# Routing stage of an encoder block on one core: when GpSimd folds, where ScalarE's exponentials and TensorE's turned picks stand

## The reference, cut to what matters

```
h    = x + mixed @ W_out;  xb = rmsnorm(h)
q    = (xb @ w_q)                                   # 8 heads x 2 halves x 64
s    = q . sub_keys                                 # 16 rows of 128 scores a token
s_top, i_top = top_k(s, 16)                         # 16 best of each row
best, pos    = top_k(sums of the two halves, 16)    # 16 best pairs a head
expert = i_top[first half] * 128 + i_top[second half] at pos
gate   = softmax(best)
```

## Time and profile before

| | |
|---|---|
| device time, median of 3 runs | 5196.68 us (5194.86 to 5203.18) |
| the profiled execution: its own time, its span | 5196.66 us, 5195.0 us |
| VectorE's first sum of `route` to its last copy on ScalarE | 2156.0 to 2702.6 us of the span |
| first marks of block 0 and of block 9 (L1968) | 2248.1 and 2677.9 us |
| from the marks of block 0 to those of block 7, a block | 49.0 us |
| blocks 8 and 9, a block | 43.5 us |

### The profile page before, as it was taken

One profiled execution on the slowest core, in us unless ns is written; L12 is line 12 of the kernel. 1 busy time (PEld: TensorE's weight loads), 2 busy tenths in 40 slices (PEclk: granted clock), 3 DMA queues, 4 the chain that ended last, 5 costly groups with the idle time before them and its releaser, 6 DMA issues. The chain is left out here.

```text
span 5195.0 us, 68977 instructions
## 1 busy us (share of the span) xinstructions
PE 4512.5 (87%) x23172; PEld 3713.1 (71%) x23172; DVE 3660.1 (70%) x7429; ACT 1535.4 (30%) x2729; POOL 2239.4 (43%) x1840
## 2 busy tenths in 40 slices
PE   7999998455599979977619679999999999999999
PEld 6888887344244448655518578889899899888898
DVE  2000000778477822288989689999999999999999
ACT  3111100455367732111109622222222222222221
POOL 4222211345245501034357555555555555665554
PEclk9999999677799989988859889999999999999999
DMA  4222211110311143200006799999999899999998
GB/s 136 82 82 82 90 61 40 51 40 10 136 62 68 42 156 120 89 33 29 29 25 183 233 352 329 339 335 339 337 336 337 318 342 337 328 326 337 333 336 295
DMA packets 376378, 978.51 MB, mean 188 GB/s; under 512 B 31097, under 2 KB 155801, under 8 KB 375961
## 3 DMA queue, kind: packets, MB, share of 16 engines
q0 software_dynamic: 156416, 575.12, 30.3%
q1 hardware_dynamic: 218688, 397.83, 22.7%
q10 hardware_dynamic: 1152, 4.19, 0.2%
HBM read 858.96 MB, written 116.75 MB: 188 GB/s over the span
## 5 line engine op out<-in xcount | busy, mean ns | idle before, releaser
L2368 PE MATMUL e_ph<-e_x,e_u 128*128 128x384 f32 x6144 | 1202.0, 337 | 67.5 <-DVE e_x L2433 52.5
L2368 PEld LDWEIGHTS e_ph<-e_x,e_u 128*128 128x128 f32 x6144 | 1097.8, 189 | 140.2 <-POOL e_u L2341 41.9
L2390 PE MATMUL e_po<-e_v,e_w 128*128 128x512 f32 x3840 | 998.4, 396 | 19.9 <-DVE e_v L2466 12.9
L2348 POOL DMA_INDIRECT e_row<-in_v_exp,expert_tok x512 | 624.7, 1220 | 468.1 <-DVE e_tok L2493 412.9
L2390 PEld LDWEIGHTS e_po<-e_v,e_w 128*128 128x128 f32 x3840 | 712.0, 188 | 140.2 <-DVE e_v L2466 13.2
L2348 POOL DMA_INDIRECT e_row<-in_u_rows,expert_tok x512 | 594.4, 1161 | 475.3 <-DVE e_row L2482 428.3
L324 PE MATMUL proj_acc<-xn,w_tile 128*128 128x512 f32 (+1 forms) x3456 | 678.1, 358 | 5.3 <-POOL w_tile L354 5.3
L2493 DVE SCALAR_TENSOR_TENSOR e_tok<-e_row,e_slot,e_tok 128x1024 f32<-128x1024 f32 x512 | 648.3, 1271 | 12.7 <-DMA e_tok<-h_tok_dram 9.2
L324 PEld LDWEIGHTS proj_acc<-xn,w_tile 128*128 128x128 f32 x3456 | 575.4, 188 | 107.8 <-POOL w_tile L354 5.5
L2482 DVE SCALAR_TENSOR_TENSOR e_row<-e_row,e_tok 128x1024 f32<-128x1024 f32 x512 | 618.9, 1213 | 7.5 <-DMA e_row<-in_u_rows,expert_tok 7.3
L284 DVE COPY proj_out<-proj_acc 128x1280 f32<-128x1280 f32 x25 | 37.3, 1492 | 659.9 <-PE proj_acc L324 647.5
(11 more groups left out here) (314 smaller groups left out, 6827.7 us busy)
## 6 DMA issues: line engine op xcount, KB each, us to landing
e_u_raw<-in_u_exp SPq DMA_DIRECT2D x128, 512.0 KB, 6.6
e_v_raw<-in_v_exp SPq DMA_DIRECT2D x128, 512.0 KB
gates_dram<-g_out SPq DMA_DIRECT2D x6, 8192.0 KB, 30.3
e_g<-gates_dram SPq DMA_DIRECT2D x128, 384.0 KB, 6.5
feat_dram<-proj_out POOLq DMA_DIRECT2D x50, 640.0 KB, 5.8
w_raw<-in_w_feat SPq DMA_DIRECT2D x50, 512.0 KB, 4.9
raw<-feat_dram SPq DMA_DIRECT2D x22, 640.0 KB, 6.1
mx_gate<-feat_dram SPq DMA_DIRECT2D x16, 640.0 KB, 4.0
```

The costliest lines, as they stand in the source:

```text
L2348: pool.indirect_dma_start(out=row[r % RB][:], out_offset=None, in_=u_rows if r < TOK_ROWS else v_rows, in_offset=bass.IndirectOffsetOnAxis ...
L2368: ins = nc.tensor.matmul(ph[q % 2][:, 0:tn], u[b][j][:, kk, :], xs[m][:, kk, t0:t0 + tn], start=(i == 0), stop=(i == 3 * DC - 1))
L2390: ins = nc.tensor.matmul(out, w[b][j][:, blk * P:(blk + 1) * P], v[2 * odd + b][m][:, half * HALF:(half + 1) * HALF], start=(n == 0 and (f ...
```

## The change

Three edits, all in `route`. GpSimd waits for both sets of marks of block n before it folds the first. ScalarE takes the exponentials of block n behind `scale_features(n + 2)` in its round n, rather than those of block n-1 at the start of the round, and copies the turned picks behind both halves of the queries. TensorE does both halves of the queries before it turns the picks. No instruction is added or removed.

```diff
                 for n in range(TB):
+                    pool.wait_ge(marked[1], n + 1)
                     for j, rows in ((0, slice(0, 8)), (1, slice(8, 16))):
                         pool.wait_ge(marked[j], n + 1)
...
                 for n in range(TB):
-                    if n:
-                        gates_of(n - 1)
                     if n + 2 < TB:
                         root(n + 2)
                         scale_rows(n + 2)
                         scale_features(n + 2)
-                        keep_queries(n + 2, 0)
+                    gates_of(n)
+                    if n + 2 < TB:
+                        for half in range(2):
+                            keep_queries(n + 2, half)
                     if n:
                         keep_turned(n - 1)
-                    if n + 2 < TB:
-                        keep_queries(n + 2, 1)
-                gates_of(TB - 1)
                 keep_turned(TB - 1)
...
                     if n + 2 < TB:
                         turn_rows(n + 2, 1)
-                        queries(n + 2, 0)
+                        for half in range(2):
+                            queries(n + 2, half)
                     if n:
                         turn(n - 1)
-                    if n + 2 < TB:
-                        queries(n + 2, 1)
                 turn(TB - 1)
```

## The result

The changed kernel takes 5104.06 us (median of 4 runs, 5103.15 to 5109.79) where the kernel before, in the same comparison, took 5195.77: a ratio of 0.9825, with a 95% interval of 0.9808 to 0.9842. The profiled execution has 5103.16 us and a span of 5101.5 us.

What follows compares the result with a forecast made beforehand. A circle of waits through TensorE, ScalarE's exponentials and VectorE, 48.81 us, was taken to bound the kernel. First to last marks 94.8 us less, 1.6 lost at the end: 93.2 off 5196.66 gives 5103.5 us, range 5093 to 5120.

Steps and rivals of the forecast that it cites:

- the circle: Waits through TensorE, ScalarE's exponentials and VectorE, 48.81 us round, set the pace of seven blocks; VectorE's marks lie outside it.
- The marks: VectorE from first marks to next block: 13.48 us, held up by GpSimd's folding; 5.85 undisturbed, freeing 7.6 a block.
- the small steps might be slow for a reason of their own: Rival for VectorE's steps at L1971: one integer operand slows them, the first edit does nothing; 5178 us, chance 0.05.
- The exponentials: On ScalarE behind the features, done 34.6 us into the block, which ends at 37 to 38: nothing waits.
- The new circle: Scores, queries, turn and its copy, then ScalarE's root: 37.6 us and some 0.1 of semaphores, giving blocks of 37.6.
- With some 3 us of idling left, I take the warm duration: TensorE's scores take 2.06 us at the higher clock; if cold, the circle grows by 1.66, in all +6.
- Waits at `over_root` of over 1 us: Sign of being wrong: VectorE waiting over 1 us at L1866 for ScalarE's root.
- rival of a slow circle: Cold scores and caught candidate sums together: blocks of 38.4 to 39.9 us, 5109 to 5120 us, chance 0.15.
- The room of GpSimd's picks: GpSimd finishes its second set 21.4 us into the block, 1.0 before VectorE's candidate sums and 1.8 before its wait for picks.
- The turn: Moving TensorE's three transposes behind both queries saves nothing; they come 7.3 us later, with ScalarE's copy and root behind.
- The end: After block 9's first marks, later folding makes the stage's last copy move up 1.6 us less.
- The rival in which folding holds up everything: GpSimd's 18.8 us of folding delay VectorE's maxima and place searches too: blocks of 55.3 us, 5263 us, chance 0.03.

Runs made afterwards that it cites:

- the two parts: Kernel before with only GpSimd waiting for both marks: 5183.19 us; kernel before with only the ScalarE and TensorE edits: 5160.68 us.
- the kernels with the early root: Changed kernel with the next block's root ahead of ScalarE's copy of the second queries, 5096.77 us, and three variants built on it: 5102.44, 5096.59, 5096.4 us.
- the turn between the halves alone: Changed kernel with the third edit undone: TensorE turns the picks, and ScalarE copies them, between the halves of the queries; 5101.11 us.
- the kernel with early root and turn between the halves: Changed kernel with root ahead of the copy of the second queries, and the turn and its copy back between the halves; 5096.59 us.
- the last kernel: As the kernel with early root and turn between the halves, but VectorE does finish(n) ahead of its second marks; 5096.4 us.

## Why the prediction was right

**What bounded the kernel.** Right, and shown: with the marks undisturbed and the circle left, VectorE waits 10.8 us a time and only the end of the stage gets shorter; with the circle broken and the marks left, the block is VectorE's own 44. Alone the two parts bring 8.5 and 31.0 us; the other 50 or so come only when both are there.

**The marks.** 5.85 us worked out, 5.81 measured; VectorE's last two blocks 35.9 against 35.75. That the small steps might be slow for a reason of their own is refuted by 0.29 us a step in every kernel in which GpSimd stood still, and 4.83 for two in the one in which it did not. The scaling of the gates kept its stall, 1.1 us for 1.22.

**The exponentials.** No wait at L1870, as said.

**The new circle.** The mechanism was right and its size off. The step is "With some 3 us of idling left, I take the warm duration": the rounds alternate instead. In the short blocks TensorE waits 3.8 to 4.4 us and the scores start at the lower level; that round ends late, which holds VectorE up in the next block but leaves TensorE only 0.5 to 2.0 us of waiting there, and that round starts warm. The blocks average 38.3 us rather than 37.6, 4.7 us in all, of the 6 that the prediction had priced for it. Waits at `over_root` of over 1 us were among its own signs of being wrong, and three came; its rival of a slow circle, with blocks from 38.4 us, came half true, since the scores were cold every other time and the candidate sums were not caught. That the late root passes the cold rounds on to VectorE is shown by the kernels with the early root, which have cold rounds and no wait there; in the last of them the scores of blocks 1 to 7 are all cold, and no block takes more than 37.5.

**The room of GpSimd's picks.** 1.0 us to the candidate sums was worked out; in the three long blocks the last pick ended 0.9 us ahead of them (2311.30 and 2312.19 in the first), but only because VectorE waited at `over_root` as well. The prediction did not see that the two waits cover each other: taking one away uncovered the other.

**The turn.** Forecast to save nothing; undoing it changes the median by 0.4 us and the stretch between the marks by 1.1.

**The end.** +1.6 was worked out, 1.5 measured.

**The sum.** 93.2 us were forecast, 88.9 of the profiled 93.5 came from the change. That the median lies within 0.6 us of 5103.5 is partly chance: the stages ahead were 4.0 us quicker in this execution, which made up for the blocks being longer.

The rival in which folding holds up everything is refuted: the place searches (L1907) have 0.283 us in the mean over all blocks, beside 18 us of folding in each:

```profile
L1907 DVE FIND_INDEX8 r_topi<-r_top,r_psc 128x8 uint32<-128x128 f32 x144 | 40.8, 283 | 0.0
...
L1857 DVE TENSOR_TENSOR r_x<-r_acc,r_x 128x1024 f32<-128x1024 f32 x7 | 8.5, 1210 | 0.0
```

This bears on the Trainium skill's page SBUF — State Buffer (Who interferes with whom), by which a VectorE instruction with at most one input in SBUF, outside the two-port modes, does not contend with GpSimd. The trace agrees, also for the row sum (L1857), with one operand in PSUM, which keeps 1.21 us right beside the folds.

## What to carry to other kernels

Draw the circle of waits before costing an edit: a stall outside it is worth nothing until the circle is broken, and breaking it is worth only the distance to the next one. When moving work on an in-order engine, look at what then stands directly ahead of the instruction that another engine waits for: here the next block's root ended up behind two copies that didn't concern it. And when one wait goes, work out anew what it had been covering, since the slack of the next buffer was measured with that wait in place.

## What the runs showed of the hardware that was not expected

In the changed kernel TensorE's granted clock alternates from round to round. Granted clock (the third figure from the end of a row, before the DMA share and GB/s) over the scores of four successive rounds:

```profile
2264.83:2268.50 3.67, 3.67 (x32) 3.50 (x32) 3.63 (x23) 1.15 (x1) 3.51 (x3) 0.50 0.49 157
2302.26:2304.32 2.06, 2.06 (x32) 1.86 (x32) 0.00 (x0) 2.04 (x3) 2.06 (x1) 1.00 0.00 0
2342.31:2345.75 3.44, 3.44 (x33) 3.32 (x33) 3.40 (x21) 1.15 (x1) 3.28 (x3) 0.55 0.28 82
2379.74:2381.80 2.06, 2.06 (x32) 1.87 (x32) 0.73 (x5) 1.82 (x3) 2.06 (x1) 1.00 0.00 0
```

After waits of 4.36 and 4.24 us the scores run at half clock, 1.2 GHz (0.50, and 0.55 where the clock rose before their end), after 0.91 and 2.04 us at 2.4 GHz. The slower round ends late, so that TensorE's next wait is short and its next round fast; but it also holds VectorE up at `over_root`, which makes the wait after that long again. The longer the lower level lasts, the longer VectorE is held up: from 2264.83 the four transposes behind the scores are slow too (1.11 us) and VectorE waits 2.60, from 2342.31 they take 0.66 and VectorE waits 1.47. That the blocks would not alternate with one level of the clock is not shown: the turn between the halves alone has a long block with cold scores (3.64 us), and a short one follows it all the same.

The wait just before the scores doesn't settle the level by itself. Two rounds of the kernel with early root and turn between the halves, after waits of 1.99 and 1.79 us, then one of the last kernel, after 2.18:

```profile
2455.07:2458.70 3.63, 3.63 (x33) 3.42 (x33) 3.59 (x21) 1.15 (x1) 3.47 (x3) 0.53 0.02 7
2492.11:2494.10 1.99, 1.99 (x33) 1.87 (x33) 1.99 (x11) 1.15 (x1) 1.91 (x2) 1.00 0.00 0
```

```profile
2453.30:2456.90 3.60, 3.60 (x32) 3.38 (x33) 3.56 (x21) 1.15 (x1) 3.44 (x3) 0.53 0.02 7
```

A wait of 1.99 us was followed by the lower level here, one of 2.04 by the higher level above; what else decides is open. In the first of these two kernels cold and warm scores alternate for five rounds and then fall out of step; in the second those of blocks 1 to 7 are all cold. In both, blocks 2 to 7 lie within 0.5 us of each other: with the root out of the way, the lower level no longer reaches them.
